# Experts of a diffusion backbone: in the second half of a superblock's first part, ScalarE splits the next weight tile before it weighs the pick instead of after

## The reference, cut to what matters

```python
def block(args):                      # per token block, 128 picks per token
    hb, eb, gb = args
    a = jnp.einsum('td,tkd->tk', hb, u_tab[eb])
    w = gb.astype(hb.dtype) * jax.nn.gelu(a, approximate=False)
    return jnp.einsum('tk,tkd->td', w, v_tab[eb])
```

## Time and profile before

| | us |
|---|---|
| median of three runs | 4219.02 (4217.18 to 4225.48) |
| span of the profiled execution | 4219.0 |
| its expert stage of layer 0, 64 superblocks | about 1087 to 2420 |
| its expert stage of layer 1, 64 superblocks | about 3240 to 4219 |

### The profile page before, as it was taken

How to read it: one execution, slowest core, us unless ns; L and a number is a source line. 1 busy time by engine, 2 the same in 40 slices (tenths; PEclk the granted TensorE clock), 3 DMA queues, 4 the chain that set the end, 5 groups by cost and what they waited for, 6 DMA issues and landing times. The chain is left out here.

```text
span 4219.0 us, 69815 instructions
## 1 busy us (share of the span) xinstructions
PE 3869.5 (92%) x23631; PEld 3337.2 (79%) x23631; DVE 3528.4 (84%) x6910; ACT 1945.1 (46%) x3599; POOL 1105.8 (26%) x1095
## 2 busy tenths in 40 slices
PE   7969989988999999999999897898868999999998
PEld 6854468877888888888888776336767999999998
DVE  5387948999799999999999966666998899999998
ACT  4367532147444444444444355654246444444443
POOL 0000000039443434434334300000046333333332
PEclk9979999869999999999999998999979999999999
DMA  5102321246899999999999821112237999999997
GB/s 194 55 17 65 89 67 46 70 123 191 326 382 364 381 364 381 370 372 370 384 366 383 333 66 46 44 45 77 68 100 247 371 369 376 369 376 369 377 368 290
DMA packets 246997, 1018.18 MB, mean 241 GB/s; under 512 B 17121, under 2 KB 115521, under 8 KB 146641
## 3 DMA queue, kind: packets, MB, share of 16 engines
q0 software_dynamic: 85296, 599.59, 36.7%
q1 hardware_dynamic: 161504, 416.31, 28.2%
HBM read 963.34 MB, written 52.43 MB: 241 GB/s over the span
## 5 line engine op out<-in xcount | busy, mean ns | idle before, releaser
L1397 POOL DMA_INDIRECT rows<-rows,pick_i x512 | 790.6, 1544 | 1156.5 <-DVE y_tok L2663 653.2
L525 PE MATMUL psA<-h_hi,split_hi 128*128 128x448 f32 (+3 forms) x2768 | 971.8, 351 | 88.8 <-DVE xT L2642 54.7
L2027 DVE TENSOR_TENSOR split_lo<-raw,split_hi 128x1024 fp32r<-128x1024 f32 x596 | 727.9, 1221 | 303.2 <-ACT split_hi L1441 296.8
L525 PE MATMUL psA<-h_lo,split_hi 128*128 128x448 f32 (+3 forms) x2768 | 952.1, 344 | 0.0
L525 PE MATMUL psA<-h_hi,split_lo 128*128 128x448 f32 (+3 forms) x2768 | 951.8, 344 | 0.0
L1441 ACT ACTIVATE split_hi<-raw 128x1024 fp32r<-128x1024 f32 x596 | 628.3, 1054 | 304.2 <-DMA raw<-expert_pairs 153.4
L525 PEld LDWEIGHTS psA<-h_hi,split_hi 128*128 128x128 f32 x2768 | 527.5, 191 | 165.6 <-issue 112.8
L2651 DVE CUSTOM_DVE_ANT_1 rows<-rows,h_wide 128x1024 f32<-128x1024 f32 x512 | 624.8, 1220 | 25.5 <-DMA rows<-rows,pick_i 23.4
L2663 DVE SCALAR_TENSOR_TENSOR y_tok<-rows,pick_w,y_tok 128x1024 f32<-128x1024 f32 x444 | 569.1, 1282 | 5.9
L525 PEld LDWEIGHTS psA<-h_hi,split_lo 128*128 128x128 f32 x2768 | 527.3, 190 | 35.6
L525 PEld LDWEIGHTS psA<-h_lo,split_hi 128*128 128x128 f32 x2768 | 527.9, 191 | 33.3
(11 more groups left out here) (344 smaller groups left out, 6321.3 us busy)
## 6 DMA issues: line engine op xcount, KB each, us to landing
raw<-expert_pairs SPq DMA_DIRECT2D x256, 1024.0 KB, 7.2
gates<-g_buf SPq DMA_DIRECT2D x22, 2048.0 KB, 8.7
raw<-tiles SPq DMA_DIRECT2D x84, 512.0 KB, 3.7
raw<-mod_tiles SPq DMA_DIRECT2D x80, 512.0 KB, 3.6
g_in<-gates POOLq DMA_DIRECT2D x32, 896.0 KB, 9.0
g_in<-gates POOLq DMA_DIRECT2D x32, 640.0 KB, 5.9
mod_w<-mod_pairs SPq DMA_DIRECT2D x8, 1024.0 KB, 19.9
rows<-rows,pick_i POOLq DMA_INDIRECT x512, 8.4
```

What stands on the lines that cost most here:

```text
L525: ins = nc.tensor.matmul(out_, lhsT, rhs, start=start, stop=stop)
L1397: nc.gpsimd.indirect_dma_start(rows[l][:, b, :], None, (rows0, rows1)[l], bass.IndirectOffsetOnAxis(pick_i[:, u:u + 1], 0))\
L2027: V.tensor_tensor(split_lo[:, n % SPLIT].rearrange("p k n -> p (k n)"), raw[:, n % RAW, :], split_hi[:, n % SPLIT].rearrange("p k n -> p ( ...
```

## The change

In the first part of a superblock's ACT order, the half c = 0 keeps its order: gelu, weigh, split, weigh. In the half c = 1 the order was gelu(1), weigh one pick, split tile base+1; it becomes gelu(1), split tile base+1, weigh one pick. The number of picks weighed there is the same (`spread[2]`, one in both layers; in layer 1 `spread[0]` is 0). Nothing else changes: no instruction is added or taken away, and DVE, PE, POOL and SP keep their orders.

```diff
--- before.py
+++ after.py
@@ -1973,9 +1973,10 @@
                 for c in range(2):
                     if s + 1 < NSUPER:
                         gelu(c, s + 1)
-                    weigh(spread[2 * c])
+                    if c == 0:
+                        weigh(spread[0])
                     split_to(min(base + c + 1, end))
-                    weigh(spread[1] if c == 0 else 0)
+                    weigh(spread[1 + c])
                 for c in range(2):
                     split_to(min(base + c + 3, end))
                     if s + 1 < NSUPER:
```

## The result

The changed kernel takes 4117.85 us in the median of four runs (4116.38 to 4120.9), the kernel before 4218.39 beside it (4217.18 to 4225.48): a ratio of 0.9757, 95% interval 0.9743 to 0.9771, 100.5 us less. The forecast was 4137 with a range of 4112 to 4184. The direction, the place and the order of size were as forecast; the gain was a fifth larger, and the time lies in the range, near its lower end. The span of its profiled execution is 4114.5 us.

What follows compares the result with a forecast made beforehand. DVE, stalled once per superblock for ACT, was taken as the bound, with PE and the DMA next. Gains of 55 us in layer 0 and 27 in layer 1 make 82: 4219 - 82 = 4137 us, range 4112 to 4184.

Steps and rivals of the forecast that it cites:

- DVE sets the pace in both layers: Expert stages: DVE bounds, standing still once per superblock for ACT's split, 1.07 us in layer 0, 1.22 in layer 1.
- The split costs nothing where it now stands, DVE's `split_lo` moves up by 1.08 us: Tile base+1, layer 0: split done before DVE's `product(1)` ends, by 1.1 us, so `split_lo` follows 1.08 us earlier without waiting.
- Up to 0.8 us of it may stay in layer 1: Layer 1: up to 0.8 us of DVE's idle before `split_lo` may remain, as DVE now waits for PE's pace.
- The weigh has cover: ACT, behind the moved split: the weigh may slip by 1.05 us; the accumulate needing it comes some 7 us later.
- PE's floors, 19.69 and 14.54: PE becomes the bound: 19.69 us per superblock in layer 0, 14.54 in layer 1, without its waits of 0.96 and 0.43.
- DVE's floor in layer 0: DVE's superblock in layer 0 without its stall: 20.65 - 1.08 = 19.57 us, a hair under PE's.
- There is about a microsecond in which DVE may drift, and gather waits are absorbed: Layer 0, before u0: DVE may drift about a microsecond unnoticed by PE, absorbing part of gather waits, 0.22 us per superblock.
- waits of dots on gathers rise: Expected sign in the profile after: DVE's dots wait for gathers above 0.22 us per superblock.
- The margins argument: Layer 0 gathers: tightest keeps its 10.3 us against 8.5 us landings; three of five lose 1.08, to no less than that.
- the DMA's: Third bound: DMA rate taken as 390 GB/s, making layer 0's superblock 20.00 us; 396 GB/s taken as about the most.
- Rival 4: More than forecast: layer 0 reaches PE's floor of 19.69 us, 4117 with layer 1's 27; beyond 4110, chance 0.05.
- Rival 1: DMA caps the gain in both layers: 4176 at 380 GB/s, 4212 at 374; chance 0.22 of ending above 4160.

Runs made afterwards that it cites:

- e8: Kernel before the change with one chunk of the products with u left out, 6 of 96 PE matmuls per superblock; 4221.4 us, ratio 1.0015.
- e3: Changed kernel with the weigh of the second half moved once more, behind the split of base+2; 4125.6 us.
- e5: Changed kernel with DVE's split of an expert tile made over 512 of its 1024 columns; 4110.8 us.
- e6: Changed kernel with one of eight chunks of the products with u left out, 6 of 96 PE matmuls per superblock; 4084.4 us.
- e10: Changed kernel with ACT's split of tile base+1 made twice over, each copy waiting for the one before; 4128.4 us.
- e11: Changed kernel with ACT's split of tile base+1 made three times over, each copy waiting for the one before; 4192.9 us.
- e7: Changed kernel with both cuts: DVE's split over half its columns and 6 of 96 PE matmuls per superblock left out; 4024.8 us.
- e9: Changed kernel once more, unchanged, as a check on the spread; 4117.1 us.

## Why the prediction was right, and where its size was off

*DVE sets the pace in both layers* was right: e8 takes work from PE and its superblocks keep their length, and the time that the change gives back is the time of DVE's stall, as far as PE allows.

*The split costs nothing where it now stands, DVE's `split_lo` moves up by 1.08 us* was right: 65.3 us of idle time became 0.8, though with 0.6 us to spare and not 1.1. *Up to 0.8 us of it may stay in layer 1*: 37.4 / 59 = 0.63 stayed, as DVE waiting for PE's pace, a third of it before another split.

*The weigh has cover* was right within what e3 can tell: a whole split later it costs no wait per superblock.

*PE's floors, 19.69 and 14.54*: measured 19.62 to 19.63 and 14.53 in steady superblocks. e5 and e6 together show that PE is the bound. DVE's floor in layer 0 was taken as 19.57; superblocks in which DVE catches up take 19.48.

*There is about a microsecond in which DVE may drift, and gather waits are absorbed*: e10 and e11 show the room, 0.6 us taken at next to no cost and, with the second copy, a stall of 1.0 us a superblock. That gather waits were absorbed is not shown apart from this, since they vary by as much from one execution to another. The sign that *waits of dots on gathers rise* above 0.22 us per superblock didn't come: they are 0.08 to 0.17. The margins argument held: at a higher rate the gathers land hardly later (8.6 us).

**The term that was mis-sized is the DMA's.** I let it cap layer 0 at 390 GB/s, 20.00 us, because I took 396 over 30 us for the best stretch of the kernel before. It wasn't quite the best, 2294 to 2324 of the same trace has 401:

```profile
2294.00:2324.00 30.00, 28.60 (x138) 25.53 (x137) 27.63 (x34) 13.58 (x26) 10.57 (x8) 1.00 1.00 401
```

And neither was a cap, they were what the kernel asked for there; e7 draws 411 over 1100 us. Layer 0 therefore reached PE's floor, 19.66 on average: (20.00 - 19.66) x 63 = 21 us more than forecast. Layer 1 gained 31.6 instead of 27, the rest from its start. 82 + 21 + 5 = 108, against 106.9 in the two stages of the profiled execution (102 in e9's), 104.5 in the span (the untouched rest took 2.4 longer) and 100.5 in the medians. Rival 4, PE's floor in both layers at 4117, is what happened; that the median came within 1 us of it is partly luck: layer 1 gained 5 us more than that, and the rest of the program and the spread of the runs took as much back. Rival 1 fell: the DMA side binds only some 4% further on (18.97 against 19.66 us). Of the Trainium skill's figures (DMA: Bandwidth & Descriptors, Specifications), the 358 GB/s share of HBM doesn't bind this core running alone, which draws 397 to 411; its fabric ceiling of 435 is not contradicted.

## What to carry to other kernels

When two engines each keep a hand-written order and hand work to each other, look in the engine that has almost no idle time for one short, regular idle per round, and in the engine that ends it for an instruction that waits for the first engine ahead of the one that is needed: if the second needs nothing of the first and the first has time to spare, swapping those two costs nothing and gives back the stall, up to where the next engine binds (here 1.2 us in layer 0, where PE and DVE end up level, but 0.5 of 1.2 in layer 1). A busy share of 99.9% on PE didn't make it the bound; taking a little work from it did the test. And a transfer rate seen in a kernel that hardly waits for transfers is its demand, not the limit: price such a bound by a kernel that starves. Where tiles come in a ring, add up the loop from a tile's release through its load back to its release, and hold it against the engines' floors: by DVE's waits, e6 lost 20 us of its expected gain in layer 1 there.

## What the runs showed of the hardware that was not expected

- With DVE and PE lightened, this core drew 411 GB/s over 1100 us and 409 over 760 us, gathers of 8 KB rows included, at a DMA share of 1.00. A share of 0.97 at 374 GB/s had not meant that only 3% more were to be had; and 1.00 was no end either, for 100 us of e7 had 418 GB/s.
- A share of 0.99 with 396 GB/s (e6, layer 1) stood beside engines that waited for loads, and still was no cap: e7 had 409 there.
- The part of the program without any edit took 1958.9 to 1970.2 us in 13 profiled executions, so a single profile doesn't settle 5 us of a 4100 us kernel; its stages do better.
